# Transformer trunk, one core: inputs also handed over transposed, first projection by weight quarters

## The reference

```python
f = swiglu(rms_norm(h, ffn1_pre_g[i]), ffn1_w_gu[i], ffn1_w_down[i])
h = h + 0.5 * rms_norm(f, ffn1_post_g[i])
...
gate = jax.nn.sigmoid(rms_norm(h, ple_pre_g[i]) @ w_ple_gate[i])
e = (p[i] @ w_ple_proj[i]) * gate
h = h + rms_norm(e, ple_post_g[i])
```

## Time and profile before

| what | us |
|---|---|
| median of three executions | 1173.87 (1173.72 to 1174.38) |
| span of the profiled execution | 1172.6 |
| median less that span, time around it | 1.3 |
| PE busy in the span | 1164.0 |
| DVE busy | 850.0 |
| ACT busy | 721.0 |

### The profile page before, as it was taken

One profiled execution on the slowest core, in us unless ns is written; L12 is line 12 of the kernel. 1 busy time (PEld: TensorE's weight loads), 2 busy tenths in 40 slices (PEclk: granted clock), 3 DMA queues, 4 the chain that ended last, 5 costly groups with the idle time before them and its releaser, 6 DMA issues.

```text
span 1172.6 us, 17196 instructions
## 1 busy us (share of the span) xinstructions
PE 1164.0 (99%) x6031; PEld 983.8 (84%) x6031; DVE 850.0 (72%) x1290; ACT 721.0 (61%) x1166; POOL 53.0 (5%) x124
## 2 busy tenths in 40 slices
PE   9999999999999999999999999999999999999997
PEld 7888888888888888888888888888888888888886
DVE  6766776977857776676787776678776677677666
ACT  7555556577755755555685655565776566565555
POOL 4000000000000000000100000010000010000002
PEclk9999999999999999999999999999999999999999
DMA  9656564654354555655556565746434446546550
GB/s 296 217 181 212 171 215 164 226 172 152 121 201 146 191 204 185 208 174 211 179 171 198 172 211 179 240 165 198 171 111 179 162 162 215 194 170 209 179 196 37
DMA packets 138655, 215.37 MB, mean 184 GB/s; under 512 B 6958, under 2 KB 97904, under 8 KB 138608
## 3 DMA queue, kind: packets, MB, share of 16 engines
q1 hardware_dynamic: 135808, 208.43, 52.6%
q10 hardware_dynamic: 2576, 6.29, 1.6%
q0 software_dynamic: 224, 0.04, 0.0%
HBM read 213.68 MB, written 1.05 MB: 183 GB/s over the span
## 4 chain that ended last, share of the span: by engine, by line
PE 99%; DMA 0%; DVE 0%; ACT 0%; issue 0%; POOL 0%; POOLq 0%; DVEq 0%; ACTq 0%
PE ps L1673 23%; PE ps L1546 19%; PE ps L1548 18%; PE ps L1547 18%; PE ps L1683 12%; PE ps L1916 3%; PE ps L1593 1%; PE ps L1925 1%; PE ps L1802 1%; PE ps L1817 1%; PE ps L1776 0%; PE ps L1788 0%; DMA raw<-in_w_ple_proj 0%; PE ps L1831 0%; PE ps L1838 0%; PE ps L1803 0%
## 5 line engine op out<-in xcount | busy, mean ns | idle before, releaser
L1106 DVE SCALAR_TENSOR_TENSOR w_lo<-raw,g_layer,w_hi 128x512 fp32r<-128x512 f32 (+1 forms) x504 | 356.3, 767 | 139.2 <-ACT w_hi L644 139.2
L644 ACT ACTIVATE w_hi<-raw,g_layer 128x512 fp32r<-128x512 f32 (+1 forms) x524 | 346.7, 732 | 113.6 <-PE ps L1683 97.0
L1673 PE MATMUL ps<-x_both,w_hi 128*128 128x512 f32 x1152 | 287.7, 392 | 0.0
L1673 PEld LDWEIGHTS ps<-x_both,w_hi 128*128 128x128 f32 x1152 | 209.3, 189 | 39.4 <-issue 0.4
L1546 PE MATMUL ps<-w_hi,x_both 128*128 128x512 f32 x576 | 231.6, 402 | 0.0
L1548 PE MATMUL ps<-w_hi,x_both 128*128 128x512 f32 x576 | 225.0, 391 | 0.0
L1547 PE MATMUL ps<-w_lo,x_both 128*128 128x512 f32 x576 | 224.4, 390 | 0.0
L1103 DVE TENSOR_TENSOR w_lo<-raw,w_hi 128x1024 fp32r<-128x1024 f32 x114 | 134.8, 1221 | 61.3 <-ACT w_hi L641 61.3
L641 ACT ACTIVATE w_hi<-raw 128x1024 fp32r<-128x1024 f32 x114 | 114.7, 1053 | 92.7 <-PE ps L1548 92.5
L1683 PEld LDWEIGHTS ps<-x_both,w_lo 128*128 128x128 f32 x1152 | 152.6, 191 | 8.4
L1683 PE MATMUL ps<-x_both,w_lo 128*128 128x256 f32 x1152 | 156.0, 283 | 0.0
(11 more groups left out here) (230 smaller groups left out, 1041.7 us busy)
## 6 DMA issues: line engine op xcount, KB each, us to landing
raw<-in_ffn_w_gu SPq DMA_DIRECT2D x170, 512.0 KB, 4.6
raw<-in_ffn_w_down SPq DMA_DIRECT2D x88, 512.0 KB, 4.0
raw<-in_w_in SPq DMA_DIRECT2D x80, 512.0 KB, 4.5
raw<-in_w_out SPq DMA_DIRECT2D x16, 512.0 KB, 4.1
raw<-in_w_ple_gate SPq DMA_DIRECT2D x16, 512.0 KB, 4.1
raw<-in_w_branch_sb SPq DMA_DIRECT2D x8, 512.0 KB, 4.1
raw<-in_w_branch_diff SPq DMA_DIRECT2D x8, 512.0 KB, 4.2
raw<-in_ffn_w_gu SPq DMA_DIRECT2D x12, 256.0 KB, 7.8
```

The lines of the kernel that those rows point to most:

```text
L644: last = act.activation(w_hi[:, s, part], raw[:, s, part], ACT.Copy, scale=g_layer[:, g:g + 1])
L1106: last = dve.scalar_tensor_tensor(out=w_lo[:, s, part], in0=raw[:, s, part], scalar=g_layer[:, g:g + 1], in1=whi[:, part], op0=ALU.mult, o ...
L1673: mm = pe.matmul(dst, w_hi[:, s, cols], x_both[:, :, 4 * half + k, :], start=half == 0 and k == 0, stop=stop and k == 3, skip_group_check= ...
```

## The change

Three arrays are added on the host: `x_t`, which is `x` transposed, `p_t`, `p` transposed, and `gains`, the norm weights as 33 columns per layer. `x` is still loaded for the residual stream, now as two 512 KB loads by SP between units 2 and 3. `x_t` comes in four 256 KB loads on ACT's queue, `x_raw[n]`, each with blocks 2n and 2n + 1 of all 256 tokens; their place in memory is that of the later query and key tiles (`sbq_t`, `sbk_t`). Written x(n) below. ACT and DVE split straight from them (`high_x`, `low_x`). The projection runs quarter by quarter, for both token tiles, and within a quarter high by high first, then the low part of `p`, then the low part of the weight. Of the transposes only the warm-up (12), and those of later inputs, are left. (The diff is cut to its core.)

```diff
         def _(sp_):
-            def load_p(t):
-                sp_.dma_start(p_nat[:, t, :], a["p"][0, 0, t * P:(t + 1) * P, :]).then_inc(p_in[t], 16)
-
-            for t in range(TT):
-                load_p(t)
+            for k in range(2):
+                sp_.dma_start(p_raw[:, k, :], a["p_t"][0, k * P:(k + 1) * P, :]).then_inc(p_in[k], 16)
 
...
 
             load_pieces(U_PROJ, (1, 3))
-            for u in range(1, PIECED):
-                load_pieces(u)
+            load_pieces(1)
+            load_pieces(2)
+            for t in range(TT):
+                sp_.dma_start(h[:, t, :], a["x"][0, t * P:(t + 1) * P, :]).then_inc(h_loaded[t], 16)
+            load_pieces(3)
             for i in range(DEPTH):
                 if i:
                     load_deep(i, U_PROJ, a["w_ple_proj"], 0)
...
         def _(pool):
+            pool.dma_start(g_all[:, :, :], a["gains"].rearrange("l p n -> p l n")).then_inc(g_in, 16)
             pool.memset(ident[:, :], 0.0).then_inc(blank, 1)
             pool.wait_ge(blank, 1)
             pool.affine_select(out=ident[:, :], in_=ident[:, :], compare_op=ALU.not_equal, fill=1.0,
                                base=0, pattern=[[-1, P]], channel_multiplier=1).then_inc(const_id, 1)
-            pool.dma_start(g_rows[0:2 * KD, :], a["ffn1_pre_g"].rearrange("l (k p) -> (l k) p", p=P)
-                           ).then_inc(first_g_in, 16)
-            for n, name in ((1, "mix_pre_g"), (2, "ffn2_pre_g"), (3, "ple_pre_g")):
-                pool.dma_start(g_rows[2 * KD * n:2 * KD * (n + 1), :],
-                               a[name].rearrange("l (k p) -> (l k) p", p=P)).then_inc(g_in, 16)
-            pool.dma_start(g_rows[64:66, :], a["diff_subln_g"]).then_inc(g_in, 16)
             for t in range(TT):
                 pool.dma_start(pos_i[:, t:t + 1], a["positions"][0, t * P:(t + 1) * P].rearrange(
...
-            def load_x(idx):
-                rows, cols = slice(idx // 2 * P, (idx // 2 + 1) * P), slice(idx % 2 * W, (idx % 2 + 1) * W)
-                act.dma_start(h[:, idx // 2, cols], a["x"][0, rows, cols]).then_inc(h_loaded[idx], 16)
+            def load_x(n):
+                act.dma_start(x_raw[n], a["x_t"][2 * n * P:2 * (n + 1) * P, :].rearrange("(k p) n -> p k n", p=P)
+                              ).then_inc(x_in[n], 16)
 
             load_x(0)
-            load_x(2)
             act.preload_act_table_set("silu_and_others")
 
...
+            def high_x(n):
+
+                act.wait_ge(x_in[n], 16)
+                act.activation(x_hi[:, 2 * n:2 * n + 2, :], x_raw[n], ACT.Copy).then_inc(x_high, 1)
+
...
                     idx = 2 * t + n
-                    act.wait_ge(x_turned, nth_x(i, q, idx))
+                    act.wait_ge(x_turned, nth_turn(i, q, idx))
...
                 act.wait_ge(h_ready, 16 * i + 4 * n + 2 * t + 2)
+                if (i, n) == (0, 0):
+                    act.wait_ge(h_loaded[t], 16)
                 act.activation(tmp[:, t, :], h[:, t, :], ACT.Square, scale=D ** -0.5,
...
                               a[name][i, :].partition_broadcast(P)
                               ).then_inc(post_in[s], 16)
 
-            high_piece(U_PROJ, 0)
-            high_p(0, 0, slice(0, P))
-            high_piece(U_PROJ, 2)
-            high_p(0, 1, slice(P, SEQ))
-            high_piece(U_PROJ, 1)
-            high_piece(U_PROJ, 3)
+            for k in (0, 2, 1, 3):
+                high_piece(U_PROJ, k)
             load_x(1)
-            high_inputs(0, 0, 0, (0,))
-            act.wait_ge(first_g, 1)
+            high_x(0)
+            act.wait_ge(layer_g, 1)
             high_piece(1, 0)
             high_piece(1, 1)
+            load_x(2)
+            high_x(1)
+            high_piece(1, 2)
+            high_piece(1, 3)
             load_x(3)
-            high_piece(1, 2)
-            high_inputs(0, 0, 1, (0,))
-            high_piece(1, 3)
+            high_x(2)
             high_piece(2, 0)
             for t in range(TT):
                 keep_e(0, t)
             high_piece(2, 1)
-            high_inputs(0, 0, 0, (1,))
+            high_x(3)
             high_piece(2, 2)
             high_piece(2, 3)
             high_piece(3, 0)
...
-                dve.wait_ge(cols_turned, 2)
-                dve.tensor_copy(g_cols[:, :, 0:DEPTH * KD], gains[1][:, 0:64].rearrange("p (n k) -> p n k", n=4))
-                dve.tensor_copy(g_layer[:, KD:4 * KD].rearrange("p (n k) -> p n k", n=3),
-                                gains[1][:, 2 * KD:8 * KD].rearrange("p (n l k) -> p n l k", n=3, l=2)[:, :, 0, :])
+                dve.wait_ge(g_in, 16)
+                dve.tensor_copy(g_layer[:, 0:32], g_all[:, 0, 0:32])
                 for n in range(DEPTH):
                     dve.memset(neg_inits[:, n:n + 1], -LAM_INIT[n])
-                    dve.tensor_scalar(g_sub[:, n:n + 1], gains[1][:, 64 + n:65 + n], 1.0 - LAM_INIT[n], None, ALU.mult)
+                    dve.tensor_scalar(g_sub[:, n:n + 1], g_all[:, n, 32:33], 1.0 - LAM_INIT[n], None, ALU.mult)
                 dve.memset(neg_init[:, :], -LAM_INIT[0])
-                dve.tensor_scalar(g_layer[:, 32:33], gains[1][:, 64:65], 1.0 - LAM_INIT[0], None, ALU.mult
+                dve.tensor_scalar(g_layer[:, 32:33], g_all[:, 0, 32:33], 1.0 - LAM_INIT[0], None, ALU.mult
                                   ).then_inc(layer_g, 1)
+                dve.wait_ge(layer_g, 1)
 
...
+            def first_p(k):
+
+                dve.wait_ge(p_in[k], 16)
+                dve.tensor_copy(p_hi[:, k, :], p_raw[:, k, :]).then_inc(p_high, 1)
+                dve.wait_ge(p_high, k + 1)
+                dve.tensor_tensor(p_lo[:, k, :], p_raw[:, k, :], p_hi[:, k, :].bitcast(F32), ALU.subtract
+                                  ).then_inc(p_split, 1)
+
+            def low_x(n):
+
+                part = slice(2 * n, 2 * n + 2)
+                dve.wait_ge(x_high, n + 1)
+                dve.tensor_tensor(x_lo[:, part, :], x_raw[n], x_hi[:, part, :].bitcast(F32), ALU.subtract
+                                  ).then_inc(x_split, 1)
+
+            first_p(0)
             low_piece(U_PROJ, 0)
-            low_p(0, 0, slice(0, P))
             low_piece(U_PROJ, 2)
-            low_p(0, 1, slice(P, SEQ))
+            first_p(1)
             low_piece(U_PROJ, 1)
             low_piece(U_PROJ, 3)
-            keep_first_gain()
-            low_inputs(0, 0, 0, (0,))
+            keep_gains()
+            low_x(0)
             low_piece(1, 0)
             low_piece(1, 1)
-            keep_gains()
+            low_x(1)
             low_piece(1, 2)
-            low_inputs(0, 0, 1, (0,))
             low_piece(1, 3)
+            low_x(2)
             low_piece(2, 0)
             low_piece(2, 1)
-            low_inputs(0, 0, 0, (1,))
+            low_x(3)
             low_piece(2, 2)
             low_piece(2, 3)
-            low_piece(3, 0)
-            low_inputs(0, 0, 1, (1,))
-            for k in range(1, 4):
+            for k in range(4):
                 low_piece(3, k)
 
...
+                if q == 0 and t == 1:
                     pe.wait_ge(e_kept[1], i + 1)
                 for k in range(4):
...
                 def wait():
+                    if k % 2 == 0:
+                        pe.wait_ge(x_split, 2 * (u - U_FFN1) + k // 2 + 1)
                     if k < 3:
                         pe.wait_ge(piece_split, 3 * u + k + 1)
                     else:
                         begin(0, u)
-                    if then:
-                        then()
                 return wait
 
...
                 def first_gate_up(s, t, before):
-                    inputs(i, q, t, s)
+                    if q or i:
+                        inputs(i, q, t, s)
                     return wide(slot(u0 + s), bank(GU_BANK[t]), x_hi, x_lo, 4 * s, t, s == 0, s == 1, before)
...
                     for s in range(2):
                         for t in range(TT):
-                            before = turned_at(0, 0, *{(0, 1): ((1,), (1,)), (1, 0): ((3,), (1,))}.get((s, t), ((), ())))
-                            if t == 0:
-                                before = {k: pieced(u0 + s, k, before.get(k)) for k in range(4)}
-                            mm = first_gate_up(s, t, before)
+                            mm = first_gate_up(s, t, {k: pieced(u0 + s, k) for k in range(4)} if t == 0 else None)
...
+            def warm_up():
+
+                for _ in range(WARM_UP):
+                    mm = pe.transpose(bank(GU_BANK[0])[:, 0:P], ident[:, :], ident[:, :])
+                mm.then_inc(units_used, SLOTS)
 
             def first_proj():
 
-                beside = {(0, 1): lambda: (turn(0, 0, 0), turn_first_gain()), (0, 3): lambda: turn(0, 0, 2),
-                          (1, 3): turn_gains}
-                for t, k in ((0, 0), (0, 2), (1, 0), (1, 2), (0, 1), (0, 3), (1, 1), (1, 3)):
-                    if (t, k) in beside:
-                        beside[t, k]()
-                    if k == 0:
```

(41 more changed lines are left out.)

102 lines of the change are left out of this document (30 added, 72 removed).

## The result

The changed kernel takes **1180.68 us** (median of five, 1178.86 to 1180.77), the kernel before 1174.18 (now five executions, 1173.72 to 1174.38): ratio 1.0053, with an interval of 1.0041 to 1.0065, about 6 us slower. The profiled execution took 1179.94 and has a span of 1178.2, 5.6 more than before. Three of the other four took 1180.68 to 1180.77, with a mean granted clock of 0.995 to 0.996 where the profiled one has 0.998. So the clock was probably low for longer in these than the trace shows.

What follows compares the result with a forecast made beforehand. PE, never idle from 24 to 1166 us, was taken as the bound. Unit 3 3.2 later, plus 0.4 for the clock, less 0.44: 3.2 later, span 1175.8, plus 1.3, 1177.0 us; range 1172.5 to 1180.5.

Steps and rivals of the forecast that it cites:

- a long wait of PE for x(1): Unit 1, before quarter 2: PE idles 3.5 us, starting that quarter at 16.9.
- the 0.44 at 551 us: Layer 1: the four transposes of `p` go, gaining 0.44 us that reaches the end.
- The rival in which the x loads overtake the backlog: Start: x(n) land 3.6 us after issue, unit 3 starts at 24.15, 1171.9 us; chance 0.12.
- `h` goes first: Rival, start: x(1) lands at 17.7 behind `h`, unit 3 starts at 30.75, 1178.5 to 1181.4 us; chance 0.17.
- x(1) issued at 8.5, landing 14.8: Load for unit 1's quarters 2 and 3, on ACT's queue; landing between ends of 12.1 and 17.7.
- 256 KB less in front: ACT's queue: with 256 KB less of `x` ahead, x(1) is issued at 8.5 instead of 9.00.
- x(2): 18.8 forecast: Load for unit 2, issued at about 10.5 to 10.9: lands at 18.8, ends 14.1 and 20.
- Waits of 3.5, 1.6 and 0.7: PE's idle times before unit 1's quarter 2 and in unit 2 around quarter 1, together 5.8 us.
- The clock, 0.4: Unit 1 after the 3.5 us idle: a fallen clock slows the 18 products left, taken as 0.4 us.
- PE found other time to lose after 30 us, which I exclude: Sign of a wrong forecast: PE losing further time behind 30 us, which was excluded.
- as forecast, the wait covered it: Projection: a late warm-up and later clock rise cost nothing; the wait found covers up to 3.5 us.
- the 1.3: End of the sum: the median time was taken to lie 1.3 us above the profiled span.

Runs made afterwards that it cites:

- h_late: Changed kernel with both 512 KB loads of `h` moved behind unit 3's quarters on SP's queue: 1179.59 us, ratio 1.0044.
- x_early: Changed kernel with x(1), x(2) and x(3) each issued one place earlier on ACT's queue: 1176.14 us, ratio 1.002.
- warm: Changed kernel with 34 transposes of the identity filling PE's wait before quarter 2 of unit 1: 1179.04 us, ratio 1.0043.

## Why the prediction was right, and where it was too low

**Right.** Direction and mechanism: a long wait of PE for x(1), a second one in unit 2, the clock falling behind the first, the 0.44 at 551 us. The rival in which the x loads overtake the backlog, which the Trainium skill's rule of going round the queues (DMA: Bandwidth & Descriptors, Queues, rings and completion order) would make the forecast, asked for x(1) at about 12.1. It came at 15.9, 6.9 us after its issue on a queue with nothing else on it, and `h_late` and `x_early` show that the place in the order of issue matters most. The trace disagrees with what I had worked out from that rule; it doesn't show how single packets were served. Some overtaking there is: in the earlier trace rows the load issued at 9.00 landed at 15.5, that of 7.78 at 16.8, and x(3) passed two loads issued 3.5 and 4.2 us before it. That `h` goes first is refuted as well: with `h` moved away x(1) lands no earlier and takes 0.8 less from its issue, not 2.9.

**Too low by 3.7** (1177.0 against 1180.7, 0.2 above the top of the range; in span +3.2 forecast, +5.6 measured). Term by term:

- *x(1) issued at 8.5, landing 14.8.* Issued at 9.01 and 6.9 in flight instead of 6.3, 15.9. The step that took half a microsecond off the old kernel's 9.00 for "256 KB less in front" failed: ACT's wait for the projection's quarter ended at the same time. From 4 to 10 us the DMA engines moved 286, 265 and 308 GB/s (in stretches of 2 us), before 402, 311 and 346. Which of the new loads does that wasn't tried. From the landing to PE's start I had 2.1, measured 2.17. x(2): 18.8 forecast, 19.85. x(3): 21.4, 21.7.
- *Waits of 3.5, 1.6 and 0.7.* PE waited 3.90 and 0.36. The slow products and a unit 1 that began 0.6 later than the 12.0 I had took up the rest.
- *The clock, 0.4.* It was at the lower level from 19.05 to 22.47. By `warm` 0.6 to 1.7.
- These make unit 3 start at 29.96 instead of 29.3 (28.9, and 0.4 for the clock): 0.7 of the 2.4 us that are missing in the span.
- *"PE found other time to lose after 30 us, which I exclude."* This is the step that failed as reasoning. 0.57 up to the turns of `glu` (the wait of 0.43 among it), 0.9 in the two mixers, and 0.2 in small steps: 1.7 in all. That PE never waits behind 24 us in the old trace shows that ACT's chain was ahead of it there, not by how much. Here ACT's chain behind x(3) was shifted too, and PE waited for it. And I had priced the new tile's size at nothing: of the 0.9 it made 0.34 in each mixer.
- The warm-up started at 3.10 (1.59 before) and the clock rose at 8.8 instead of 7.3; as forecast, the wait covered it.
- The median lies 2.5 above the profiled span where I took 1.3: 0.7 because the profiled execution (1179.94) was faster than the median, and 0.5 because the 1.3 was too low. The time of an execution is 1.7 to 1.8 above its own span in every run here; before, the profiled execution was itself 0.5 slower than the median.

**What the change is worth.** Its pieces: 0.44 from the turns of `p`; up to 1.7 at unit 3 from the turns of `x`, if its loads go in order of need; -0.7 in the products on `os_hi` and `os_lo`, and about -1 in all, from the address; nothing measurable from high parts first. The second read of `x` is 1 MB at full DMA engines, an estimated 2.9 us. Where these bytes stand decides most: 1180.68 as it was written, 1175.15 with `x` in order of need. The runs that came out faster than before (1172.23 and 1172.0) have the address put right, `h` in order of need and the silu ahead of the weights as well. Whether the silu's move alone would help the kernel before wasn't tried; there PE waits for nothing between 24 and 1166 us, so nothing in its trace asks for it.
